# Local attention by half-array products on TensorE, and more dummy products in a large single-core kernel

## The reference, cut to what matters

```python
def window_attention(q, k, v, kc, vc, sink):
    ...
    kb, vb = band(k), band(v)
    ...
    s_band = jnp.einsum('bkgnqd,bknsd->bkgnqs', qb, kb).astype(jnp.float32) * scale
    s_band = jnp.where(valid, s_band, NEG_INF)
    s_ctx = jnp.einsum('bkgnqd,bksd->bkgnqs', qb, kc).astype(jnp.float32) * scale
    ...
    p = softmax_with_sink(jnp.concatenate([s_band, s_ctx], axis=-1), sink_b).astype(v.dtype)
    o = (jnp.einsum('bkgnqs,bknsd->bkgnqd', p[..., :3 * BLOCK], vb)
         + jnp.einsum('bkgnqs,bksd->bkgnqd', p[..., 3 * BLOCK:], vc))
```

## Time and profile before

| | |
|---|---|
| median of three runs | 4063.89 us (4057.85 to 4063.95) |
| profiled execution, its own time | 4055.57 us |
| its span, first to last instruction | 4053.8 us |
| mean granted TensorE clock | 0.977 |
| TensorE matmul busy | 3824.3 us, 94% of the span |
| VectorE, ScalarE, GpSimd busy | 40%, 35%, 28% |
| chain of work that ended last | TensorE 79%, VectorE 8%, ScalarE 5% |

### The profile page before, as it was taken

How to read it: one execution, slowest core, us unless ns; L and a number is a source line. 1 busy time by engine, 2 the same in 40 slices (tenths; PEclk the granted TensorE clock), 3 DMA queues, 4 the chain that set the end, 5 groups by cost and what they waited for, 6 DMA issues and landing times.

```text
span 4053.8 us, 52334 instructions
## 1 busy us (share of the span) xinstructions
PE 3824.3 (94%) x22125; PEld 3161.7 (78%) x22125; DVE 1621.4 (40%) x2600; ACT 1408.8 (35%) x2209; POOL 1147.2 (28%) x689
## 2 busy tenths in 40 slices
PE   7999889999999899897999999999998889999999
PEld 5777667888887677676888788888877766688887
DVE  4355573111136666666212321111457843332123
ACT  4223344211125433434422332211455536443223
POOL 2010013111123423425222421211434413243324
PEclk9999999999999999999999999999999999999999
DMA  5221123332333121123333412222322210152333
GB/s 181 73 80 32 58 92 122 97 96 92 96 104 87 33 67 47 33 63 130 107 105 101 151 53 67 64 63 60 117 72 67 59 44 29 55 151 73 99 95 108
DMA packets 472117, 336.66 MB, mean 83 GB/s; under 512 B 17754, under 2 KB 445772, under 8 KB 471884
## 3 DMA queue, kind: packets, MB, share of 16 engines
q1 hardware_dynamic: 471200, 333.06, 27.0%
q10 hardware_dynamic: 683, 0.26, 0.0%
HBM read 331.17 MB, written 2.10 MB: 82 GB/s over the span
## 4 chain that ended last, share of the span: by engine, by line
PE 79%; DVE 8%; ACT 5%; POOL 3%; DMA 2%; issue 2%; SPq 0%; ACTq 0%; POOLq 0%; DVEq 0%
PE PS L107 77%; DVE A L124 2%; PE PS L115 1%; POOL TM L124 1%; ACT A L118 1%; ACT L118 1%; DVE A L132 1%; POOL RWr L124 1%; DMA MW<-in_w_ada 1%; ACT RWH L121 1%; DMA MW<-in_mod_w 1%; DVE TM L132 1%; DVE XT L124 1%; DVE SM L144 1%; ACT TM L118 0%
## 5 line engine op out<-in xcount | busy, mean ns | idle before, releaser
L124 POOL TENSOR_TENSOR RWr<-RW,RWH 128x1024 fp32r<-128x1024 f32 (+2 forms) x316 | 728.4, 2307 | 2235.8 <-ACT RWH L121 2233.1
L107 PE MATMUL PS<-HTH,RWH 128*128 128x512 f32 (+1 forms) x3488 | 1262.7, 362 | 20.8 <-POOL RWr L124 7.6
L107 PE MATMUL PS<-HTH,RWr 128*128 128x512 f32 (+1 forms) x3488 | 1228.1, 352 | 0.0
L107 PE MATMUL PS<-HTr,RWH 128*128 128x512 f32 (+1 forms) x3488 | 1227.9, 352 | 0.0
L107 PE MATMUL PS<-Ar,RWH 128*128 128x512 f32 (+1 forms) x3264 | 819.6, 342 | 20.2 <-DVE XT L132 7.1
L107 PEld LDWEIGHTS PS<-HTH,RWH 128*128 128x128 f32 x3488 | 665.9, 191 | 144.2 <-issue 43.9
L107 PEld LDWEIGHTS PS<-HTr,RWH 128*128 128x128 f32 x3488 | 666.4, 191 | 89.5 <-issue 6.5
L107 PEld LDWEIGHTS PS<-HTH,RWr 128*128 128x128 f32 x3488 | 664.9, 191 | 90.6 <-issue 0.4
L107 PEld LDWEIGHTS PS<-Ar,RWH 128*128 128x128 f32 x3264 | 563.8, 191 | 108.4 <-issue 18.1
L121 ACT ACTIVATE RWH<-RW 128x1024 fp32r<-128x1024 f32 (+2 forms) x474 | 474.8, 1006 | 310.7 <-DMA RW<-in_ffn_w_out 164.9
L107 PE MATMUL PS<-Ar,RWr 128*128 128x512 f32 (+1 forms) x1632 | 552.8, 339 | 0.0
(11 more groups left out here) (189 smaller groups left out, 3403.5 us busy)
## 6 DMA issues: line engine op xcount, KB each, us to landing
RW<-in_ffn_w_in SPq DMA_DIRECT2D x176, 512.0 KB, 3.8
MW<-in_mod_w SPq DMA_DIRECT2D x83, 512.0 KB, 4.6
MW<-in_w_ada SPq DMA_DIRECT2D x72, 512.0 KB, 4.5
RW<-in_ffn_w_out SPq DMA_DIRECT2D x64, 512.0 KB, 3.6
RW<-in_ffn_w_out SPq DMA_DIRECT2D x64, 384.0 KB, 3.2
RW<-in_mix_w_in SPq DMA_DIRECT2D x41, 512.0 KB, 3.7
RW<-in_ssd_w_in SPq DMA_DIRECT2D x40, 512.0 KB, 3.9
RW<-in_ev_w_in SPq DMA_DIRECT2D x24, 512.0 KB, 3.8
```

What stands on the lines that cost most here:

```text
L107: return self._ins(self.real and self.real.matmul(o, l, r, start=start, stop=stop, skip_group_check=True))
L124: return self._ins(self.real and self.real.tensor_tensor(out=o, in0=i0, in1=i1, op=op))
```

## The change

**Value products.** `vv` holds the values once. For each key block there are two matmuls in place of one: one of 64 columns of values against the 256 columns of the two even heads, into partitions 0 to 63, and one for the two odd heads into partitions 64 to 127. ScalarE's copy into `vv` is one in place of two.

**Scores.** In an even slot TensorE now issues the scores of units t and t+1 together, four banks for both, alternating by key block between the units, hence between the row halves. In an odd slot it issues none. VectorE and ScalarE keep their steps; they now wait for the pair's semaphore.

**Dummy products.** The table has 87 more of them in 25 places, 13 of which had none before.

```diff
-        self.vv = al(1536).rearrange("p (c v d n) -> p c v d n", c=6, v=2, d=2)
+        self.vv = al(768).rearrange("p (c v n) -> p c v n", c=6, v=2)
...
         elif step == "score":
-            n, h = self.units[a[0]]
-            r, kv = slice(64 * (h % 2), 64 * (h % 2) + 64), h // 4
-            lq = self.q[r, h // 2, n * 128:n * 128 + 128]
-            pv = k.banks.take(p, 2, "win", "score", *a)
-            p.wait_ge("v.win_rope", max(h // 2, 1))
-            for x, c in self.keys(n)[:-2]:
-                at = 128 * x if x < 2 else 512
-                p.mm(pv[:, at:at + 128], lq, self.kk[r, kv, c * 128:c * 128 + 128], True, True)
-            p.mm(pv[:, 640:896], lq, self.kk[r, kv, 512:768], True, True).then_inc("pe.win", "score", *a)
+            if a[0] % 2:
+                return
+            pair = (a[0], a[0] + 1)
+            for u in pair:
+                k.banks.take(p, 2, "win", "score", u)
+            p.wait_ge("v.win_rope", max(self.units[a[0]][1] // 2, 1))
+            for x, c in self.keys(self.units[a[0]][0])[:-1]:
+                for u in pair:
+                    n, h = self.units[u]
+                    r, kv, pv = slice(64 * (h % 2), 64 * (h % 2) + 64), h // 4, k.banks.of("win", "score", u)
+                    at, wide = (128 * x if x < 2 else 512, 128) if c < 4 else (640, 256)
+                    last = p.mm(pv[:, at:at + wide], self.q[r, h // 2, n * 128:n * 128 + 128],
+                                self.kk[r, kv, c * 128:c * 128 + wide], True, True)
+            last.then_inc("pe.win", "score", a[0] // 2)
...
             for x, c in keys:
-                last = p.mm(pv[:, 0:512], self.vv[:, c, kv, :, :].rearrange("p d n -> p (d n)"),
-                            self.wt[g % 2][:, x, :, :].rearrange("p j n -> p (j n)"), x == keys[0][0], x == keys[-1][0])
+                for b in range(2):
+                    last = p.mm(pv[64 * b:64 * b + 64, 0:256].rearrange("p (a n) -> p a n", a=2), self.vv[:, c, kv, :],
+                                self.wt[g % 2][:, x, :, :].rearrange("p (a b) n -> p a b n", a=2)[:, :, b, :],
+                                x == keys[0][0], x == keys[-1][0])
...
-            for d in range(2):
-                made = s.copy(self.vv[:, :, :, d, :].rearrange("p c v n -> p (c v) n"), pv)
-            made.then_inc("s.win_in", "vt").frees("win", "vt")
+            s.copy(self.vv.rearrange("p c v n -> p (c v) n"), pv).then_inc("s.win_in", "vt").frees("win", "vt")
...
-        'MixOut m00': {('mix', 3, None): 3},
+        'MixOut m00': {('mix', 2, None): 6, ('mix', 3, None): 3},
...
-        'Pre b1': {('var', H0, 0): 6, ('var', H1, 0): 6},
+        'Pre b1': {('var', H0, 0): 8, ('var', H1, 0): 8},
...
-        'Window': {('rope', 1): 6, ('score', 0): 7, ('wt', 4): 3, ('wt', 23): 4, ('wt', 26): 3, ('wt', 27): 3, ('wt',
+        'Window': {('rope', 1): 8, ('score', 0): 11, ('wt', 3): 3, ('wt', 4): 3, ('wt', 10): 3, ('wt', 23): 4, ('wt', 26): 3, ('wt', 27): 3, ('wt',
             30): 4, ('wt', 31): 3},
```

More of the change, by code:

```diff
@@ L3226, in result @@
         n, kv, r = g % 4, g // 4, slice(64 * b, 64 * b + 64)
-        pv = self.k.banks.of("win", "value", g)[r, 0:512].rearrange("p (a b n) -> p a b n", a=2, b=2)[:, :, b, :]
+        pv = self.k.banks.of("win", "value", g)[r, 0:256].rearrange("p (a n) -> p a n", a=2)
         return *(x[r, 2 * kv:2 * kv + 2, n * 128:n * 128 + 128] for x in (self.OAH, self.OAL)), pv
@@ L3252, in vector @@
                 v.wait_ge("g.win_n", t - 3)
-            v.wait_ge("pe.win", "score", t)
+            v.wait_ge("pe.win", "score", t // 2)
             v.tt(ev[:, lo:hi], pv[:, lo:hi], self.WM.rearrange("p d n -> p (d n)")[:, lo:hi], ALU.add).then_inc("v.step")
@@ L3731, in plan @@
         'Gla 0': {('q', 0): 4, ('v', 0): 3},
-        'MixOut m00': {('mix', 3, None): 3},
+        'MixOut m00': {('mix', 2, None): 6, ('mix', 3, None): 3},
         'Gla 1': {('fold', 3): 3},
-        'Diff': {('value', 3): 3, ('pc', 'v', 3, 0, 0): 3, ('value', 13): 9, ('wt', 20): 4, ('fold', 3, X): 3},
+        'Diff': {('pc', 'v', 1, 0, 0): 3, ('value', 3): 5, ('pc', 'v', 3, 0, 0): 5, ('value', 13): 12, ('wt', 20): 4, ('fold', 3, X): 3},
         'Mod': {('row', 58): 6, ('turn', 11): 2, ('row', 107): 3, ('row', 111): 3, ('turn', 15): 2, ('row', 133): 3,
-            ('row', 142): 4, ('row', 147): 4, ('row', 166): 4},
+            ('row', 142): 4, ('row', 147): 4, ('row', 166): 7},
         'Head 0 ssd dt': {('tile', X, 0): 4},
-        'Head 0 f1 gate': {('tile', H0, 0): 10},
+        'Head 0 f1 gate': {('tile', H0, 0): 14},
         'Head 0 b2 gate': {('tile', H0, 0): 6},
@@ L3741, in plan @@
         'Ssd': {('z', 0, 0, 0): 2, ('z', 2, 0, 0): 2, ('z', 3, 0, 0): 2, ('ctr', 1, 5): 3, ('ctr', 2, 5): 3, ('ctr', 3,
-            5): 3, ('st', 0, 0, 0): 2, ('st', 1, 0, 0): 2, ('st', 2, 0, 0): 2, ('st', 3, 0, 0): 2, },
-        'Pre b1': {('var', H0, 0): 6, ('var', H1, 0): 6},
-        'LayerNorm e1': {('mean', H1): 4},
-        'Pre mix2': {('var', X, 1): 3, ('var', C, 0): 11},
+            5): 3, ('st', 0, 0, 0): 2, ('st', 1, 0, 0): 2, ('st', 2, 0, 0): 2, ('st', 3, 0, 0): 2, ('yd', 0, 1): 5, ('yd', 0, 3): 4, ('yd', 1, 1): 4, ('yd', 1, 3): 5, ('gp', 2, 1): 3,
+            ('yd', 2, 1): 3, ('yd', 2, 3): 4, ('yd', 3, 1): 5},
+        'Pre b1': {('var', H0, 0): 8, ('var', H1, 0): 8},
+        'LayerNorm f0': {('mean', X): 3},
+        'LayerNorm e1': {('mean', H1): 8},
+        'Pre mix2': {('var', X, 1): 3, ('var', C, 0): 16},
         'Hgrn': {('vt', 0): 4, ('l2', 0, 1, 3): 3, ('l2', 0, 1, 6): 5, ('l2', 1, 1, 6): 5, ('l2', 2, 1, 6): 5, ('l2', 1,
@@ L3748, in plan @@
             4, ('l2', 3, 1, 1): 4, ('l2', 3, 1, 2): 3, ('l2', 3, 1, 3): 3, ('l2', 3, 1, 5): 2, ('l2', 3, 1, 6): 3},
[1 row of a table removed]
[1 row of a table added]
             30): 4, ('wt', 31): 3},
         'Merge': {('y', 0, H0): 2},
-        'Pre b2': {('var', H1, 0): 5},
+        'Pre b2': {('var', H1, 0): 8},
     }
```

## The result

The kernel after takes 3997.36 us (median of four runs, 3996.84 to 3999.40), the kernel before on the same chip 4063.92 (4057.85 to 4065.87). The gain between the medians is 66.6 us; the ratio of the runs is 0.9845 with a 95% interval of 0.9831 to 0.9859, which is 57 to 69 us. I predicted 4022, with a range down to 4002. The profiled execution took 3997.38 us. Two runs of the last round, at far lower clocks than all others (e12_after 14219.97 us, e15_ten 4260.3 us), are left out of the numbers here.

The account below looks back on a forecast made before the run. TensorE, busy 94% of the span, was taken to bound the kernel. Local attention -24, dummy cost +4 and clock -18 made -38 us on 4055.6, so 4018; with half of 8.3 added, 4022 us, range 4002 to 4043.

Parts of the forecast that it names:

- I take 18: Clock gain from the new dummies: 18 us taken, with bounds 0 and 42.
- What of it counts: Local attention: of 31.3 us less TensorE work, 3.5, 1 and 3 are lost, leaving 24 us gained.
- 17 waits: Waits that get dummies; low-clock stretches behind them total 91 us, TensorE busy 84.8; 42 us if all went high.
- rival 2: The clock falls somewhere else instead, so dummies gain nothing from it: 4040 us, 12% chance.
- last slots: End of the local attention, said to be led by the other engines; 3.5 us of the gain lost there.
- slots 4 to 7: Local attention slots said to wait for GpSimd and VectorE too; 1 us of the gain lost.
- new waits: Local attention: pairs need four banks at once, gate halves may wait on ScalarE; +3 us taken, bounds -5 and +10.
- rival 1: Local attention becomes a chain of ScalarE and VectorE, half of its gain: 4034 us, 21% chance.
- rival 4: The array halves do not overlap here, so the change does not do what it says: 4046 us, 4% chance.
- ten without cover: Ten of the 87 added dummies have no idle time to fill; cost 4.4 us, taken as 4.
- Rival 5: Dummies wait for a bank and run in front of the real step, 38 us cost: 4074 us, 4% chance.
- Rival 3: Everything comes through, the full 31 us and 33 of the 42 from the clock: 4000 us, 9% chance.

Follow-up runs that it names:

- e12_after: The kernel after, unchanged, run again on the chip of the last four experiments; 3995.66 us, ratio 0.9843 to the kernel before.
- e15_ten: The kernel after without ten of its 87 added dummy products, those counted as standing beside no wait; 3991.10 us, ratio 0.9832 to the kernel before.
- e3_both: The kernel before with value products and scores changed, the table of dummies as before; 4021.79 us, ratio 0.9912.
- e7_apart: Values and scores changed, old table, but a pair's units issued one after the other with a small all-row product between; 4055.08 us, ratio 0.9977 to the kernel before.
- e10_over: The kernel after with four more dummies at each of eight places of the state-space mixer, 32 in all; 4006.64 us, ratio 0.9862 to the kernel before.
- e4_table: The kernel before with the new table of dummies alone, products as before; 4034.98 us, ratio 0.9936.
- e6_vouter: The kernel after, value products issued as all key blocks of one column half, then the other; 3996.97 us, ratio 0.9838 to the kernel before.
- e5_outer: The kernel after, scores of a pair issued unit after unit with nothing between; 3999.42 us, ratio 0.9844 to the kernel before.

## Why the prediction was wrong

**Two steps failed, both discounts: "I take 18" for the clock, and "What of it counts" for the local attention.** Dummies and clock together gave 22.5 us and not 14, the local attention 35.7 and not 24.

**The clock.** I took 18, out of 42 for 91 us behind 17 waits. What came off is 184.5 - 122.6 = 62 us of low clock, worth 22 to 27 us and at most 31; the table alone took 73 us away (184.5 to 111.7). It went where the forecast puts it: with 3 us on either side of the 17 stretches, the same work has 89 us of low clock before and 9.5 after. In the other traces with the new table it has 3 to 27 us there, in those with the old one 44 to 80. I had two arguments for less than half. The first, that 1 to 2 us of idle time stay and the clock may fall as behind 3381.38, holds at 207.85. But at 2936 no idle time is left, at 3596 it is 0.59 us, and at the eight places of the state-space mixer 0.6 to 1.5, with the clock high behind each. The second, that work at the low clock only lengthens until the next wait, is right in kind, but it takes only a fifth: 0.36 to 0.43 us for each us of low clock where a full TensorE would have 0.5. Nor did the clock fall elsewhere instead (rival 2). Away from the 17 stretches there are 94 us before and 111 after, and in twelve traces, five of them with the old table, it is anywhere from 84 to 135: chance.

**The local attention came whole.** The sizes of the work were right: 14.9 us for the value products, as predicted to the tenth, and 18.8 for the scores where I took 16.4 from the factor of the differential attention; the two row halves give 1.98, not 1.77. Wrong was "What of it counts", which took 7.5 of the 31.3 off: 3.5 for the last slots, 1 for slots 4 to 7 and 3 for new waits. At equal clock the stage of e3_both, with the two changes alone, is 35.7 us shorter, 2 us more than the work that went. The last slots are 10 us shorter with as much idle time as before. An idle TensorE there did not mean that another engine led: the chain goes through TensorE and back, with 62% of it on TensorE. The new waits are one of 2.38 us, against 5.2 us of waits that went, which I had read as one in every second slot. Of rival 1 (a chain of ScalarE and VectorE) nothing is seen in the slots with gate halves beyond that one wait, and rival 4 (the halves do not overlap) is excluded by the start times and by e7_apart.

**The dummies' cost.** I took 4 us, for ten without cover. No run measures it by itself. The two medians of the ten differ by 4.6 us (e15_ten against e12_after, on one chip), within the spread. With half of the low clock as its price the stretches outside of the local attention are 6.4 us longer in the kernel after and 7.9 with the table alone, and the local attention 2 and 0.7; with 0.36 to 0.43 the whole cost in the kernel after is 0 to 4 us. The 4 lies in that range. Rival 5 (dummies late) did not happen; at the places of e10_over the overfilled dummies cost about half of the price.

**The starting point.** I added half of the 8.3 us by which the profiled execution was below the median. The kernel after has no such difference, so the 4 us were lost too.

The terms with their measured sizes: 4055.6 - 35.7 - 22.5 = 3997.4 us. The 22.5 is what is left of the whole difference; the medians of e4_table have 23.5 on their own. The miss of 24.6 us is 11.7 of local attention, 8.5 of clock and dummies and 4 of the starting point, which make 24.2. Rival 3, "everything comes through" at 4000 us, was nearest, with 31 and 29 us for the two; I gave it 9%.

The Trainium skill (TensorE: Matmul & The Clock Gate, Part 3: Packing small matmuls) led to an estimate of 1.55 for two halves and 24.7 us. The kernel shows 1.88 and 1.90 for column halves, 1.98 for row halves, and 33.7 us of work that went. The drain at a change of tiling mode that the Trainium skill states (TensorEngine Tiling (Array Packing), Key Properties) agrees with the traces, and is small. The same place before, five transposes ahead of the first value product (its start is in the earlier trace rows):

```profile
3345.19 0.74 PE L115 MATMUL PS<-CC,A 128*128 128x128 f32 x5 [0.75 <-POOL A L124]
```

They take 3345.77 - 3345.19 = 0.58 us ahead of a product in the whole array and 3330.80 - 3330.13 = 0.67 ahead of one in column halves. From the last transpose alone it is 0.11 us before and 0.20 after in seven of the eight value products (the eighth waits), and 0.20 in both kernels ahead of scores without a wait. A turn to half-array products so costs 0.09 us here, 0.7 us for the eight value products.

## What to carry to other kernels

Where TensorE is above 90% busy, as here, count work that leaves it in full, also in stretches where it idles a little, and low clock that leaves it at about 0.4 us for each us; a further discount needs a row in which another engine has no slack, or the chain through that stretch. Put the two halves of the array in alternation in program order: one half after the other keeps only part of the overlap. Filling idle time with dummies cost little here even when it was overfilled, but the gain is small beside the luck of one execution (the kernel before ran from 4043 to 4080 us), so judge it by medians on one chip and read the mechanism from the changed place alone.

## What the runs showed of the hardware that I had not expected

- Products in different halves start out of program order, within limits. In e6_vouter the product of five key blocks at 3339.44 has ten records in the first column half, some 0.22 us apart; the first record of the other half starts at 3340.80, beside the seventh of the first (3340.79). Three are then left. In its product of four key blocks and in the pair of e5_outer the second chain also starts with three records of the first left. So far ahead, and no further, the other half is reached in these cases. The records do not name their half; that the two interleaved chains are the two halves is my reading. That is why two products against two, in the differential attention, overlap nearly in full though they stand unit after unit, and five against five do not.
- One kernel differs by 13 us between two chips, one round on each (3991.1 and 4004.7 us), while the kernel before differs by 3 (4063.4 and 4060.2). The clock differs with it: 0.986 to 0.987 in the runs of one, 0.983 to 0.984 in those of the other.
- Within one chip the time of a kernel follows its mean clock: in the runs of the kernel before, from 4043.6 to 4079.9 us as the clock went from about 0.980 to 0.970, 0.01 for 36 us between these two; a straight line through its 62 runs on four chips has 30. If TensorE were full all through the low stretches, 0.01 would be worth (0.01 x 4060) = 41 us.
